# One attention stage on TensorE: values as the stationary operand in column halves, the inverted sums turned instead of the output

## The reference

```python
def one_block(qi):
    s = jnp.einsum('bqkgd,bskd->bkgqs', qi, k) * scale
    p = jax.nn.softmax(s, axis=-1)
    return jnp.einsum('bkgqs,bskd->bqkgd', p, v)
...
mixed = jnp.concatenate([rmsnorm(attn, g_attn_out[l]), rmsnorm(tok, g_tok_out[l])], axis=-1)
x = x + gt1 * (mixed @ w_out[l])
```

## Time and profile before

| | |
|---|---|
| median of 3 runs | 737.26 us (737.23 to 737.5) |
| profiled execution, its own time | 737.35 us |
| its span in the trace | 735.4 us |
| PE busy, of the span | 721.1 us, 98% |
| DVE, ACT busy | 586.2 us (80%), 469.0 us (64%) |
| granted TensorE clock, mean | 0.999 of 2.4 GHz |

### The profile page before, as it was taken

One profiled execution on the slowest core, in us unless ns is written; L12 is line 12 of the kernel. 1 busy time (PEld: TensorE's weight loads), 2 busy tenths in 40 slices (PEclk: granted clock), 3 DMA queues, 4 the chain that ended last, 5 costly groups with the idle time before them and its releaser, 6 DMA issues.

```text
span 735.4 us, 14308 instructions
## 1 busy us (share of the span) xinstructions
PE 721.1 (98%) x5265; PEld 663.8 (90%) x5265; DVE 586.2 (80%) x880; ACT 469.0 (64%) x793; POOL 150.4 (20%) x151
## 2 busy tenths in 40 slices
PE   8999999999999999999999999999999999999996
PEld 7999999999999799888988877997889999999895
DVE  7999989855976587876686998998698889866667
ACT  7778775678765474555545548778686555555565
POOL 5000000021333042342232320010003121333330
PEclk9999999999999999999999999999999999999999
DMA  7664443354555859898787892963337775666551
GB/s 280 184 190 159 157 133 121 117 164 144 188 176 181 302 191 408 295 306 304 244 286 255 265 319 73 340 230 119 106 116 244 240 234 179 189 188 195 172 172 58
DMA packets 48082, 151.20 MB, mean 206 GB/s; under 512 B 9600, under 2 KB 11656, under 8 KB 48024
## 3 DMA queue, kind: packets, MB, share of 16 engines
q1 hardware_dynamic: 46184, 146.62, 60.0%
q10 hardware_dynamic: 1840, 3.80, 1.4%
HBM read 147.73 MB, written 1.06 MB: 202 GB/s over the span
## 4 chain that ended last, share of the span: by engine, by line
PE 88%; DVE 4%; ACT 3%; DMA 1%; issue 1%; SPq 1%; ACTq 0%; DVEq 0%
PE ps L881 30%; PE ps L538 21%; PE ps L814 21%; PE ps L1127 1%; PE ps L1187 1%; ACT wh L1241 1%; DVE wl L1856 1%; PE ps L669 1%; PE ps L1076 1%; DMA qrot<-qg 1%; PE ps L688 1%; PE ps L595 1%; DMA vtk<-in_x 1%; PE ps L954 1%; SPq L484 1%
## 5 line engine op out<-in xcount | busy, mean ns | idle before, releaser
L1856 DVE TENSOR_TENSOR wl<-raw,wh 128x1024 fp32r<-128x1024 f32 x220 | 282.6, 1291 | 78.9 <-ACT wh L1241 77.2
L1241 ACT ACTIVATE wh<-raw 128x1024 fp32r<-128x1024 f32 x220 | 231.5, 1055 | 62.4 <-PE ps L814 47.5
L881 PE MATMUL ps<-xh,wh 128*128 128x256 f32 x656 | 184.8, 282 | 0.0
L881 PE MATMUL ps<-xh,wl 128*128 128x256 f32 x656 | 183.8, 280 | 0.0
L881 PE MATMUL ps<-xl,wh 128*128 128x256 f32 x656 | 183.8, 280 | 0.0
L881 PEld LDWEIGHTS ps<-xh,wh 128*128 128x128 f32 x656 | 123.6, 188 | 3.8 <-issue 1.7
L881 PEld LDWEIGHTS ps<-xl,wh 128*128 128x128 f32 x656 | 123.5, 188 | 1.9
L881 PEld LDWEIGHTS ps<-xh,wl 128*128 128x128 f32 x656 | 123.7, 189 | 0.0
L538 PE MATMUL ps<-xh,wh 128*128 128x256 f32 (+2 forms) x400 | 116.9, 292 | 0.0
L538 PE MATMUL ps<-xh,wl 128*128 128x256 f32 (+2 forms) x400 | 113.2, 283 | 0.0
L538 PE MATMUL ps<-xl,wh 128*128 128x256 f32 (+2 forms) x400 | 113.0, 283 | 0.0
(11 more groups left out here) (443 smaller groups left out, 1244.6 us busy)
## 6 DMA issues: line engine op xcount, KB each, us to landing
raw<-in_w_stream SPq DMA_DIRECT2D x220, 512.0 KB, 3.9
ada_w<-in_w_ada SPq DMA_DIRECT2D x48, 512.0 KB, 6.1
vtk<-in_x SPq DMA_DIRECT2D x2, 512.0 KB, 4.6
tg_m<-in_ln_rows ACTq DMA_DIRECT2D x2, 512.0 KB, 7.1
out<-ob SPq DMA_DIRECT2D x4, 256.0 KB, 2.0
u<-uT SPq DMA_DIRECT2D x16, 34.0 KB, 2.5
eepp<-in_s_mats SPq DMA_DIRECT2D x1, 512.0 KB
decay_rows<-decay_dram SPq DMA_DIRECT2D x4, 128.0 KB
```

Of the source, the lines that this page charges most:

```text
L881: mm = nc.tensor.matmul(ps[:, bank, 0:SEQ], w, x, start=(k == 0), stop=(k == 3 * KD - 1))
L1241: nc.scalar.activation(wh[:, b % RING], raw[:, b % RING], ACT.Identity).then_inc(hi_done, 1)
L1856: V.tensor_tensor(wl[:, b % RING], raw[:, b % RING], wh[:, b % RING].bitcast(F32), ALU.subtract).then_inc(lo_done, 1)
```

## The change

Pairs of heads now use banks 6, 7 and 4, 5 in turn for scores and, in place, for the turned probabilities. `weigh_v` has the values stationary (64 columns) and the turned probabilities moving (256 columns): 4 matmuls, the two heads in the two column halves, output already turned. The inverted sums are spread over columns by DVE, turned by PE (`spread_sums`), copied by ACT (`sums_copy`) and multiplied in by DVE. The squares of the attention branch are taken per pair by ACT, added by DVE and summed over partitions by PE (`branch_ms(1)`). `lo` of block 2 moves from the QKV stage to block 0, those of blocks 3 and 4 one place later; `hi` of blocks 4 and 5 go behind the pair's exponentials and copies.

```diff
+def head_bank(h):
+    return 6 - 2 * (h // 2 % 2) + h % 2
...
PE
-            def tok_ms():
-                pe.wait_ge(S["tok_sum"], 1)
+            def branch_ms(branch):
+                pe.wait_ge(S["squares_summed"], branch + 1)
                 for t in range(NT):
+                    mm = nc.tensor.matmul(ps[:, 2 + branch, 300 + t:301 + t], sq[:, QT * (1 - branch), t * P:(t + 1) * P],
+                                          cst[:, C_ONE:C_ONE + 1], start=True, stop=True)
...
             def scores(i):
+                elif i == 1:
+                    pe.wait_ge(S["mod_done"], ADA_LOOP + 1)
                 else:
-                    pe.wait_ge(S["exp_done"], 2 * i)
+                    pe.wait_ge(S["pt_copied"], 3 * i - 4)
...
+            def spread_sums(i):
+                pe.wait_ge(S["sums_inverted"], i + 1)
+                if i == 1:
                     pe.wait_ge(S["q_std"], 3)
                     pe.wait_ge(S["branch_std"], NT)
                 elif i >= 2:
+                    pe.wait_ge(S["ao_done"], i - 1)
                 for t in range(NT):
+                    mm = nc.tensor.transpose(ps[:, 3 - i % 2, SEQ + t * P:SEQ + (t + 1) * P], ao[:, i, t * P:(t + 1) * P], ident)
+                mm.then_inc(S["o_done"], 1)
+
+            def weigh_v(i):
+                pe.wait_ge(S["pt_copied"], 3 * i + 3)
+                for s in range(NT):
                     for n in range(2):
+                        mm = nc.tensor.matmul(ps[64 * n:64 * n + 64, 3 - i % 2, 0:SEQ], vtok[:, s, 64 * (i // 2):64 * (i // 2) + 64],
+                                              probt[:, n, s, :], start=(s == 0), stop=(s == NT - 1), skip_group_check=True)
                 mm.then_inc(S["o_done"], 1)
-            def turn_attended(i):
...
             for n in range(QT):
+                if n == QT - 1:
+                    spread_sums(n)
                 pe.wait_ge(*lo_made(B_OUT2 + n))
...
                 mm.then_inc(blk_done, 1)
+                if n < QT - 1:
+                    spread_sums(n)
...
                 weigh_v(n)
-                if n >= 1:
-                    turn_attended(n - 1)
...
                 rows_in(b, mh[:, k, :], ml[:, k, :], ATT_BANKS, first=(k == 0))
                 if k == 0:
-                    turn_attended(QT - 1)
+                    branch_ms(1)
ACT
             def probt_copy(h):
                 if h >= 2:
-                    act.wait_ge(S["o_done"], h // 2)
+                    act.wait_ge(S["o_done"], h // 2 * 2)
+            def sums_copy(i):
+                act.wait_ge(S["o_done"], 2 * i + 1)
+                nc.scalar.copy(ao[:, i, :], ps[:, 3 - i % 2, SEQ:2 * SEQ]).then_inc(S["pt_copied"], 1)
             def att_hi(i):
-                act.wait_ge(S["ao_turned"], i + 1)
+                act.wait_ge(S["ao_done"], i + 1)
+                nc.scalar.activation(sq[:, i, :], ao[:, i, :], ACT.Square)
+                nc.scalar.activation(mh[:, i, :], ao[:, i, :], ACT.Identity, scale=col("g_attn", i)).then_inc(S["branch_hi"], 1)
...
-                if b < B_F2 - 1:
+                if b < B_F2 - 1 and n not in (1, 2):
                     hi(b + AHEAD)
                 if n < 3:
                     exps(2 * n + 2)
-                    exps(2 * n + 3)
                 if n < 4:
                     probt_copy(2 * n)
                     probt_copy(2 * n + 1)
+                if n < 3:
+                    exps(2 * n + 3)
+                if n < 4:
+                    sums_copy(n)
+                if n in (1, 2):
+                    hi(b + AHEAD)
...
                 if n == 5:
+                    act.wait_ge(S["branch_ms"], 2)
...
DVE
+            def invert_sums(i):
+                dve.wait_ge(S["exp_done"], 2 * i + 2)
+                r = ssum[:, 2 * i:2 * i + 2, :]
+                step(V.reciprocal(r, r))
+                V.tensor_copy(ao[:, i, :].rearrange("p (t h e) -> p t h e", t=NT, h=2),
+                              r.rearrange("p h t -> p t h")[:, :, :, None].to_broadcast([P, NT, 2, HD])).then_inc(S["sums_inverted"], 1)
             def attended(i):
+                dve.wait_ge(S["o_done"], 2 * i + 2)
+                V.tensor_tensor(ao[:, i, :], ps[:, 3 - i % 2, 0:SEQ], ao[:, i, :], ALU.mult).then_inc(S["ao_done"], 1)
...
-                if n >= 3:
+                if 3 <= n < 13:
                     lo(B_IN2 + n + AHEAD)
...
                 if n < 3:
                     maxima(2 * n + 2)
                     maxima(2 * n + 3)
+                if n < QT:
+                    invert_sums(n)
+                if n == 2:
+                    lo(b + AHEAD - 1)
                 if n == 0:
                     q_finish(n + 3)
+                    lo(b + AHEAD - 1)
...
                 if 1 <= n < 5:
                     attended(n - 1)
+                if n in (3, 4, 5):
+                    dve.wait_ge(S["branch_hi"], QT + n - 1)
+                    add = V.tensor_tensor(sq[:, 0, :], sq[:, 0, :], sq[:, n - 2, :], ALU.add)
+                    if n == 5:
+                        add.then_inc(S["squares_summed"], 1)
                 if n in (2, 3, 4, 5):
                     att_lo(n - 2)
-                if b < B_F2 - 2:
+                if n == 1:
+                    lo(b + AHEAD - 1)
+                elif n and b < B_F2 - 2:
                     lo(b + AHEAD)
```

More of the change, by code:

```diff
@@ L1110, in _ @@
                     swap_k()
-                    tok_ms()
+                    branch_ms(0)
                     q_stat(1)
@@ L1663, in exps @@
                 for t in range(NT):
-                    nc.scalar.activation(prob[:, h % 2, t, :], ps[:, 6 + h % 2, t * SEQ:(t + 1) * SEQ], ACT.Exp,
+                    nc.scalar.activation(prob[:, h % 2, t, :], ps[:, head_bank(h), t * SEQ:(t + 1) * SEQ], ACT.Exp,
                                          bias=smax[:, h, 1, t:t + 1], scale=q_scale[:, h // 2, t, h % 2:h % 2 + 1],
@@ L1674, in probt_copy @@
                 if h >= 2:
-                    act.wait_ge(S["o_done"], h // 2)
-                nc.scalar.copy(probt[:, h % 2, :, :].rearrange("p s t -> p (s t)"), ps[:, 4 + h % 2, :]).then_inc(S["pt_copied"], 1)
+                    act.wait_ge(S["o_done"], h // 2 * 2)
+                nc.scalar.copy(probt[:, h % 2, :, :].rearrange("p s t -> p (s t)"), ps[:, head_bank(h), :]).then_inc(S["pt_copied"], 1)
+            def sums_copy(i):
+                act.wait_ge(S["o_done"], 2 * i + 1)
+                nc.scalar.copy(ao[:, i, :], ps[:, 3 - i % 2, SEQ:2 * SEQ]).then_inc(S["pt_copied"], 1)
             def q_std(first):
@@ L1746, in _ @@
                     nc.scalar.activation(std[:, 0:1], eps[:, 0:1], ACT.Sqrt)
-                if n == 4:
-                    act.wait_ge(S["ao_done"], QT)
                 if n == 5:
+                    act.wait_ge(S["branch_ms"], 2)
                     for t in range(NT):
-                        square_sum((sq[:, 2 * t:2 * t + 2, :].rearrange("p a (b t) -> p (a b) t", t=P), ao[:, :, t * P:(t + 1) * P]), ss[:, t:t + 1])
-                    for t in range(NT):
-                        nc.scalar.activation(branch_rstd[:, NT + t:NT + t + 1], ss[:, t:t + 1], ACT.Sqrt, bias=eps[:, 2:3], scale=1.0 / (QT * P))\
+                        nc.scalar.activation(branch_rstd[:, NT + t:NT + t + 1], ps[:, 3, 300 + t:301 + t], ACT.Sqrt, bias=eps[:, 2:3], scale=2.0)\
                             .then_inc(S["branch_std"], 1)
@@ L2465, in maxima @@
                 dve.wait_ge(S["s_done"], h + 1)
-                step(V.tensor_reduce(smax[:, h, 0, :], ps[:, 6 + h % 2, :].rearrange("p (t s) -> p t s", t=NT), AX.X, ALU.max))
+                step(V.tensor_reduce(smax[:, h, 0, :], ps[:, head_bank(h), :].rearrange("p (t s) -> p t s", t=NT), AX.X, ALU.max))
                 V.scalar_tensor_tensor(smax[:, h, 1, :], smax[:, h, 0, :], -1.0, q_scale[:, h // 2, :, h % 2], ALU.mult, ALU.mult)\
                     .then_inc(S["max_done"], 1)
-            def attended(i):
[L2472 to L2478, removed]
+            def invert_sums(i):
[4 more added lines that the diff above has]
+                              r.rearrange("p h t -> p t h")[:, :, :, None].to_broadcast([P, NT, 2, HD])).then_inc(S["sums_inverted"], 1)
+            def attended(i):
+                dve.wait_ge(S["o_done"], 2 * i + 2)
+                V.tensor_tensor(ao[:, i, :], ps[:, 3 - i % 2, 0:SEQ], ao[:, i, :], ALU.mult).then_inc(S["ao_done"], 1)
             def att_lo(i):
                 dve.wait_ge(S["branch_hi"], QT + i + 1)
-                V.scalar_tensor_tensor(ml[:, i, :], ps[:, 2 + i % 2, SEQ:2 * SEQ], col("g_attn", i), mh[:, i, :].bitcast(F32),
+                V.scalar_tensor_tensor(ml[:, i, :], ao[:, i, :], col("g_attn", i), mh[:, i, :].bitcast(F32),
                                        ALU.mult, ALU.subtract).then_inc(S["branch_lo"], 1)
@@ L2573, in _ @@
                     attended(n - 1)
+                if n in (3, 4, 5):
[3 more added lines that the diff above has]
+                        add.then_inc(S["squares_summed"], 1)
```

(7 more changed lines are left out.)

28 lines of the change are left out of this document (4 added, 24 removed).

## The result

The changed kernel takes 740.51 us (median of 5 runs, 739.89 to 741.07) against 737.5 us of the kernel before beside it (737.23 to 738.08). The medians lie 3.0 us apart. The ratio is 1.0037, with a 95% interval of 1.0027 to 1.0048: slower by 0.37%, 2.7 us. The profiled execution took 740.78 us over a span of 739.0 us, 3.6 us more than the span before.

What follows compares the result with a forecast made beforehand. PE was taken as the bound (98% busy), ACT a close second. Block 4 0.4 us ahead and 2.7 us lost at `branch_ms(1)` gave +2.3 us, hence 739.5 us; own case 738.8 to 740.2, stated range 737.1 to 740.8.

Steps and rivals of the forecast that it cites:

- three waits: New PE waits: before the turn of pair 3's sums (2.8 us), block 4 (1.0 us) and `branch_ms(1)` (2.45 us).
- the forecast's own case: Whole kernel: +2.3 us from the schedule, 739.5 us, within 738.8 to 740.2; chance 0.61.
- the serial column halves: Rival at `weigh_v`: column halves run one after the other, 1.9 us each, kernel 740.7 us; chance 0.07.
- The product: `weigh_v` on PE: 4 matmuls of 256 columns take 0.95 us instead of 1.73.
- ACT's list: ACT from `exps(2)` at 498.9 to pair 0's high part at 516.4: packed, starts 1.15 us earlier, ends as before.
- First wait: PE before `spread_sums(3)`, ahead of block 3: waits about 2.8 us for DVE's inversion and spreading, done by 519.1.
- Second wait: PE before block 4: waits some 1.0 us for both gated parts after block 3; block 4 starts at 524.3.
- Third wait: PE at `branch_ms(1)`, between blocks 4 and 5: waits 2.45 us for the last square behind `hi` of block 8; 2.7 us lost.
- Sum: To the end of the first quarter: -0.4 us at block 4 plus 2.7 us at `branch_ms(1)`, +2.3 us.
- The clock: Rival: PE idles 2.8 and 2.5 us in new waits, a block at 1.2 GHz takes 2.9 us more, 742.4 us; chance 0.04.
- The faster rival: PE's sum decides: pair 3's inversion reached by 516.3, block 4 starts at 521.1, net -0.9 us, 736.4 us; chance 0.11.

Runs made afterwards that it cites:

- e9: The changed kernel itself, run again unaltered beside the kernel with two sized fillers on the same chip; 741.24 us.
- e1: The changed kernel with `branch_ms(1)` moved on PE from behind block 4 to behind block 5; 738.47 us.
- e2: The changed kernel with inversion and spreading of pair 3's sums moved on DVE from behind `lo` of block 5 to behind pair 1's product; 743.06 us.
- e4: The changed kernel with 18 identity matmuls on PE in front of the turn of pair 3's sums; 742.68 us.
- e11: The three-move kernel with PE's second gated-parts wait only ahead of block 4's second token tile, residual additions behind pair 3's low part; 734.31 us.

## Why the prediction held, point by point

The three waits were forecast where they are, and without a fall of the clock their sum comes out within 0.1 us. That the measured 740.51 us lies in the stated range is partly luck: the forecast's own case was given 738.8 to 740.2, and the upper bound of 740.8 took in the serial column halves (740.7), a rival that is false.

- *The product.* Forecast 0.95 us, measured 1.01. The column halves overlap, as line 975 had said; the serial rival is out.
- *ACT's list.* Forecast: `exps(2)` at 498.9, high part of pair 0 at 516.4. In the trace 498.90 and 516.40. The second isn't ACT's list alone, though: ACT is idle for 0.47 us up to 514.86, waiting for PE's turn of the third pair's sums, which the forecast hadn't in it; other pieces were that much shorter.
- *First wait.* Forecast 2.8 us, the turn passing at 519.2; measured 2.31 in the bracket, the turn at 519.02, PE idle from 516.7, 0.4 us later than figured. The spreading copy took 0.29 us, not 0.43.
- *Second wait.* Forecast 1.0 us, measured 0.58, since block 3 ended late: DVE was idle for 1.14 us ahead of the first gated part, waiting for it. Without the fall (e9) it is 0.89 us, and block 4 starts at 524.19, forecast 524.3.
- *Third wait.* Forecast 2.45 us in front of `branch_ms(1)` and 2.7 us lost between the starts of blocks 4 and 5. Measured 2.37, and 5.86 (525.39 to 531.25) against 3.02 us: 2.84. The pieces of the wait, which the prediction adds up from rows of the kernel before, came out as figured. Moving the instruction (e1) gave 2.0 us back in the median and 2.7 us in the stage, where both traces have one fall.
- *Sum.* +2.3 us was forecast for the schedule alone. With fillers that keep the clock the span is 2.3 us longer, and in the profiled execution of e9, which had no fall, 737.8, 2.4 us longer; the stage by itself (39.16 against 36.83) 2.3 us.
- *The clock, the term that was left out.* I gave the fall a chance of 0.04, on the ground that PE was idle from 729 to 733 at a granted clock of 1.00, "so 2.8 us seem safe". The rows stop 1 us short. In the same idle piece, which begins with PE's last matmul at 728.99, the clock does fall, at 733.9:

```profile
733.00:734.00 1.00, 0.00 (x0) 0.00 (x0) 0.00 (x0) 0.00 (x0) 0.00 (x0) 0.95 0.83 311
734.00:735.00 1.00, 0.00 (x0) 0.00 (x0) 0.00 (x0) 0.00 (x0) 0.00 (x0) 0.50 0.59 221
```

  The inference was wrong as well: in the stage the clock fell only when PE was back at work, so a stretch of idle time at full clock says nothing on what follows it. The fall stands in the profiles of the changed kernel, of e1, e2 (twice) and e4. It makes a block 1.3 to 1.6 us longer; in the changed kernel 1.2 us of that reach the span (739.0 against 737.8 us). The rule of the Trainium skill (TensorE: Matmul & The Clock Gate, on why it matters for kernels) that idle gaps between bursts can cost the full clock, which I had set against rows 6, agrees with this case for five of the nine gaps of 2.3 to 2.5 us; behind the other four the clock stayed full. The rival's price, 2.9 us, was too high, since only part of the block ran slow.
- *What the medians hold besides.* The forecast's 739.5 us started from 737.26; the kernel before took 737.5 beside the changed one, which is 0.2 us of the 1.0 missing. The rest isn't simply the fall. The median execution (740.51 us, span 738.6) has a mean granted clock of 0.999 and so can't have had one; it is 0.8 us longer than the profile without a fall. A late arrival at the stage would do that, but this execution has no trace, and the cause stays open. In e9 four of the five executions, 741.11 to 741.95 us, have means of 0.995 or 0.996, and there one fall or more is likely.
- *The faster rival* needed the inversion 2 us earlier. Where e2 gave just that, block 4 started at 523.35, not 521.1: the gated parts stood behind `lo` of block 6. It took three moves to have it.

## What to carry to other kernels

Where every engine's list is written by hand and nearly full, a change that takes work off the bounding engine can be worth nothing until each new wait is followed to the instruction that it stands behind in another engine's list: here three moves within the lists turned a loss of 0.37% into a gain of 0.36%, without changing what is computed. Look for a small result, needed late, whose consumer stands early (`branch_ms(1)` between two blocks), and for a wait put on a whole block that only half of it needs. Treat an idle piece such as those of 2.3 to 2.5 us here as dearer than its length, since the clock may fall behind it: remove it or fill it, and fill it no longer than it is. And when two profiled executions are compared, measure the stage from a mark ahead of it: here the arrival alone moved by up to 1.3 us.

## What the runs showed of the hardware that I had not expected

- In the stage the granted clock fell after the idle time, not in it: PE idle 516.7 to 519.0, clock at 0.50 from shortly after 519.8 to about 523.1, with PE working. In one of the two profiled executions of the same program it fell, in the other not. In the longer idle time at the program's end it fell while PE was idle (last matmul over at 728.99, clock at 0.50 from 733.9 in the kernel before).
- DVE's 256-column instruction with two SBUF inputs takes 0.94 to 1.06 us instead of 0.48 while POOL adds. The Trainium skill (GPSIMD Engine Reference, Specifications) names such contention of the two engines for DVE instructions with two SBUF inputs; the trace agrees. The gated part at 520.55, which reads one of its two tiles from PSUM, met POOL's addition too (520.50) and took 0.75 us, as in e11 without it.
- A float32 matmul of 128 by 128 columns is two instructions and 0.23 us in a row of its like (18 in 4.21 us).
- The time at which the program reaches the stage varies by up to 1.3 us between profiled executions, and the stage moves with it. In the traces looked at for this it comes from waits for DMAs, the first of them for the input: 4.22, 4.65 and 4.90 us.
